# Small TensorE products as two 64-column halves in a 2-block transformer kernel, and a later start of GpSimd's first weight sums

## The reference, cut to what matters

```python
def layer_norm(x, g, b):
    ...
    y = (xf - mu) * lax.rsqrt(var + LN_EPS) * g + b

# RWKV-7 in chunks of 128 tokens, per head (8 heads of 64): with L a masked 128x128
# matrix (row t uses tokens s before t, or up to t),
#   Z = L1 @ V (+ state part),  U = X @ Z,  Y = L2 @ U + L3 @ V (+ state part)

mod = jax.nn.silu(c) @ w_ada + b_ada              # shift2 enters the router as a constant
logits = h2 @ w_router                            # = ... + shift2 @ w_router, the same for all tokens
out = rms_norm_2(x, final_norm_g)                 # needs the sum of squares of each token
```

## Time and profile before

| | |
|---|---|
| median of the runs | 2457.34 us |
| the profiled execution | 2456.72 us |
| its span, first to last instruction | 2454.9 us |
| TensorE busy | 2294.8 us, 93% of the span |
| VectorE, ScalarE, GpSimd busy | 28%, 16%, 16% |
| mean granted TensorE clock | 0.988 |

### The profile page before, as it was taken

One profiled execution on the slowest core, in us unless ns is written; L12 is line 12 of the kernel. 1 busy time (PEld: TensorE's weight loads), 2 busy tenths in 40 slices (PEclk: granted clock), 3 DMA queues, 4 the chain that ended last, 5 costly groups with the idle time before them and its releaser, 6 DMA issues.

```text
span 2454.9 us, 28556 instructions
## 1 busy us (share of the span) xinstructions
PE 2294.8 (93%) x12460; PEld 1536.5 (63%) x12460; DVE 675.2 (28%) x1192; ACT 401.5 (16%) x780; POOL 389.3 (16%) x347
## 2 busy tenths in 40 slices
PE   9999999999999999999888888899999998888878
PEld 8766676676667888987333333378889863333324
DVE  4543224433215644212100000034443221000001
ACT  3310112521014321111100000033112020000001
POOL 2377631258742000000000000000000000000000
PEclk9999999999999999999999999999999999999999
DMA  7377732358742332238999999953333599999997
GB/s 269 115 288 288 305 128 86 110 214 343 298 165 75 108 138 87 104 137 353 412 429 427 428 427 428 415 183 113 113 104 103 201 394 429 427 428 427 428 426 315
DMA packets 136504, 654.61 MB, mean 267 GB/s; under 512 B 9784, under 2 KB 14776, under 8 KB 107832
## 3 DMA queue, kind: packets, MB, share of 16 engines
q1 hardware_dynamic: 136376, 652.71, 66.8%
HBM read 651.64 MB, written 1.05 MB: 266 GB/s over the span
## 4 chain that ended last, share of the span: by engine, by line
PE 72%; DMA 22%; DVE 3%; ACT 1%; issue 1%; SPq 0%; POOL 0%; DVEq 0%; ACTq 0%
PE bank L719 71%; DMA PRGT<-in_w_exp_up 9%; DMA ring<-in_w_exp_up 6%; DMA PRGT<-in_w_exp_down 4%; DMA ring<-in_w_exp_gate 3%; DVE R L1876 1%; ACT R L3055 1%; SPq L639 0%; DVE stat L1857 0%; PE bank L1277 0%; DMA ring<-in_hy_w_in 0%; DVE sm L2002 0%; POOL PRGT L3153 0%; ACT SQ L3095 0%; PE bank L897 0%
## 5 line engine op out<-in xcount | busy, mean ns | idle before, releaser
L719 PE MATMUL bank<-hT,ring 128*128 128x256 f32 x3392 | 759.2, 382 | 7.7 <-ACT hT L2699 7.7
L719 PEld LDWEIGHTS bank<-hT,ring 128*128 128x128 f32 x3392 | 640.7, 191 | 114.9 <-issue 18.6
L719 PE MATMUL bank<-PRGT,R 128*32 128x512 f32 x1120 | 288.8, 608 | 39.2 <-DMA PRGT<-in_w_exp_up 33.1
L719 PE MATMUL bank<-ring,R 128*32 128x512 f32 (+1 forms) x960 | 263.5, 596 | 32.6 <-DMA ring<-in_w_exp_up 17.8
L3229 POOL TENSOR_TENSOR SQ<-xT 128x512 f32<-128x512 f32 x4 | 4.2, 1041 | 1513.9 <-DVE xT L2672 1513.8
L719 PE MATMUL bank<-PRGT,SQ 128*32 128x512 f32 (+2 forms) x896 | 192.0, 533 | 16.1 <-ACT SQ L3095 12.2
L719 PEld LDWEIGHTS bank<-PRGT,R 128*32 128x32 f32 x1120 | 77.6, 112 | 183.1 <-issue 182.6
L719 PEld LDWEIGHTS bank<-ring,R 128*32 128x32 f32 (+1 forms) x960 | 73.2, 114 | 179.6 <-issue 179.3
L719 PE MATMUL bank<-PRGT,ring 128*128 128x256 f32 (+4 forms) x1040 | 175.9, 372 | 0.0
L719 PE MATMUL bank<-ring,SQ 128*32 128x512 f32 (+2 forms) x552 | 161.9, 556 | 8.3 <-ACT SQ L3095 8.3
L719 PEld LDWEIGHTS bank<-PRGT,ring 128*128 128x128 f32 (+3 forms) x1040 | 145.1, 170 | 28.0 <-issue 2.2
(11 more groups left out here) (387 smaller groups left out, 2158.4 us busy)
## 6 DMA issues: line engine op xcount, KB each, us to landing
PRGT<-in_w_exp_gate SPq DMA_DIRECT2D x36, 2048.0 KB, 31.9
PRGT<-in_w_exp_up SPq DMA_DIRECT2D x34, 2048.0 KB, 31.8
ring<-in_mlp_w SPq DMA_DIRECT2D x32, 2048.0 KB, 9.2
PRGT<-in_w_exp_down SPq DMA_DIRECT2D x32, 2048.0 KB, 32.1
ring<-in_w_exp_up SPq DMA_DIRECT2D x30, 2048.0 KB, 31.9
ring<-in_w_exp_gate SPq DMA_DIRECT2D x28, 2048.0 KB, 32.6
PRGT<-in_w_ada SPq DMA_DIRECT2D x32, 1536.0 KB, 11.3
ring<-in_w_exp_down SPq DMA_DIRECT2D x22, 2048.0 KB, 31.9
```

The lines of the kernel that those rows point to most:

```text
L719: return mm(o, lhsT=lhsT, rhs=rhs, start=first, stop=last, **kw)
```

## The change

Four things are done. (1) Each product of the recurrence with a triangular matrix becomes two, by `causal`: the first takes source rows 0 to 63 and writes output rows 0 to 63 (64x64 weights), the second takes all 128 source rows and writes output rows 64 to 127 (weights of 128 rows and 64 columns). The corner of `XT` is then never read, and its memset goes. (2) The 8 products of `rconst` become 16, with 64 weight columns each, to the lower and the upper half. (3) So do the 12 of `sums_by_token`. (4) GpSimd's `weight_sums(l, 0)` waits until VectorE has scaled the eighth tile of the layer norm.

```diff
+                def causal(o, h, lhs, rhs, start, stop, **more):
+
+                    for half in range(2):
+                        src, dst = slice(0, 64 + 64 * half), slice(64 * half, 64 * half + 64)
+                        ins = mul(o[dst, h * 64:h * 64 + 64], lhs[src, place(h) * P + 64 * half:place(h) * P + 64 * half + 64],
+                                  rhs[src, :], start, stop, **more)
+                    return ins
...
                     for h in range(RW_H):
-                        ins = mul(o[:, h * 64:h * 64 + 64], NT[c][:, place(h) * P:(place(h) + 1) * P],
-                                  VT2[:, c * 512 + h * 64:c * 512 + h * 64 + 64], h == 0, False, skip_group_check=True)
+                        ins = causal(o, h, NT[c], VT2[:, c * 512 + h * 64:c * 512 + h * 64 + 64], h == 0, False, skip_group_check=True)
...
                     for h in range(RW_H):
-                        ins = mul(o[:, h * 64:h * 64 + 64], XT[c][:, place(h) * P:(place(h) + 1) * P], Zm[:, h * 64:h * 64 + 64])
+                        ins = causal(o, h, XT[c], Zm[:, h * 64:h * 64 + 64], True, True)
...
-                        hs, hp = slice(h * 64, h * 64 + 64), slice(place(h) * P, (place(h) + 1) * P)
-                        mul(o[:, hs], RB[c][:, hp], Um[:, hs], h == 0, False, skip_group_check=True)
-                        ins = mul(o[:, hs], RK[c][:, hp], VT2[:, c * 512 + h * 64:c * 512 + h * 64 + 64], False, False,
-                                  skip_group_check=True)
+                        causal(o, h, RB[c], Um[:, h * 64:h * 64 + 64], h == 0, False, skip_group_check=True)
+                        ins = causal(o, h, RK[c], VT2[:, c * 512 + h * 64:c * 512 + h * 64 + 64], False, False, skip_group_check=True)
...
                 for k in range(KT):
-                    mul(o[:, 0:36], mod[:, 48 * l + 24 + k:48 * l + 25 + k].to_broadcast([P, P]), wr[:, k, :], k == 0, False)
+                    for half in (slice(0, 64), slice(64, 128)):
+                        mul(o[half, 0:36], mod[:, 48 * l + 24 + k:48 * l + 25 + k].to_broadcast([P, 64]), wr[:, k, :], k == 0, False)
...
                     for tt in range(TT):
-                        ins = mul(acc[3][:, tt:tt + 1], SQ[:, k, tt * P:(tt + 1) * P], C("ones")[:, 0:1],
-                                  first and k == 2 * t and tt == 0, last and k == 2 * t + 1, skip_group_check=True)
+                        for half in (0, 64):
+                            ins = mul(acc[3][half:half + 64, tt:tt + 1], SQ[:, k, tt * P + half:tt * P + half + 64], C("ones")[:, 0:1],
+                                      first and k == 2 * t and tt == 0, last and k == 2 * t + 1, skip_group_check=True)
...
-                for c in range(TT):
-                    v.memset(h8(XT[c])[64:128, :, 0:64], 0.0)
...
                 s, u = SLOT_AT[f"mlp{l}"][2 * (q % 4 // 2) + 1]
                 pool.wait_ge(slot_full[s], loaded(u, q // 4))
+                if q == 0:
+                    pool.wait_ge(sems["norm_scaled"], (8, 30)[l])
```

## The result

The changed kernel takes 2508.77 us (median of 4 runs, 2508.01 to 2508.93), the kernel before 2457.89 beside it (4 runs, 2455.5 to 2461.85). The ratio is 1.021, with a 95% interval of 1.0197 to 1.0222: 2.1% or 51 us slower. The forecast was 2490, with a range up to 2502. The direction was right, and so was the mechanism of the products and of the norms. The loss by TensorE's clock was taken far too small; the forecast was off by 19 us in all, and the time lies 7 us outside the range.

What follows compares the result with a forecast made beforehand. TensorE was taken to bound the kernel, with 72% of the span. 2456.7 + 41.1 (products) + 3 (clock) - 9.7 (norms) - 1.3 (`rconst`) - 0.5 (token sums) = 2489.3, plus 0.6 for the median: 2490 us, range 2437 to 2502.

Steps and rivals of the forecast that it cites:

- What bounds it: Whole span: 72% TensorE, 22% DMA; a later recurrence moves the experts' stage as a whole and hides nothing.
- The products, +41.1: Recurrence: 256 records become 256 halves at 0.26 us, +38.9, plus entries and exits; ends +35.9 and +61.5 us.
- The edges (entry and exit): Between 12 stretches of recurrence products and the big projections: 0.2 us each, less what chunk 0 pays, +2.2 us.
- rival (A): Recurrence: halves of different height run side by side on separate columns, 0.031 us per record; kernel 2436 us; chance 0.18.
- (B): Recurrence: a shape change costs something between, near 0.145 us per half, paid for by the norms; about 2457 us; chance 0.04.
- The clock, +3 with bounds 0 and +10: Recurrence's four 16-product stretches, 8.3 us each: two falls to half clock, each costing up to 1.7 us.
- if the clock falls in all four long stretches: Recurrence's 16-product stretches: named as the next way to fail, after the price of a shape change.
- The layer norms, -9.7: First norm of each layer: scalings without GpSimd beside them gain 3.65 us in the first layer, 6.04 in the second.
- rival (C): Layer norms: products as forecast, but the norms don't speed up; 2500 us; chance 0.04.
- GpSimd's sums had slack: First layer norm: GpSimd's delayed weight sums cost nothing, ending 1.4 us before its row sums could start.
- The small ones: `rconst` in halves -1.3 us over both layers, token sums -0.5 us, removed memsets worth nothing.
- The sum: Whole kernel: profiled 2456.7 us plus all terms gives 2489.3; median of runs 0.6 higher, 2490 us, 1.3% slower.

Runs made afterwards that it cites:

- the wait alone: Only GpSimd's wait for the layer norm's last scaled tile added to the kernel before; 2447.77 us, ratio 0.9965.
- the last version: The changed kernel, but both halves of each triangular product take all 128 source rows and the memsets stay; 2433.61 us, ratio 0.9907 against the kernel before.
- by turns: Only the recurrence's products in alternating halves of 64 and 128 source rows, memsets gone, against the kernel before; 2517.26 us, ratio 1.024.
- half as many changes of shape: Only the recurrence's products in 64- and 128-source-row halves, their order reversed in every second head, against the kernel before; 2499.07 us, ratio 1.0168.
- sorted: Only the recurrence's products halved, all 64-row halves of a stretch before all 128-row ones, against the kernel before; 2463.71 us, ratio 1.0022.

## Why the prediction was right, and where it was wrong

**What bounds it.** Right. The recurrence is one piece of TensorE, and what it lost moved all behind it; the experts' stage kept its length within 1.4 us (449.5 and 450.9 us from norm to norm in layer 1; 451.2 and 449.9 in layer 2, of which the last token sums are 0.7).

**The products, +41.1.** Right. At full clock a half costs 0.257 us (0.514 a product), forecast at 0.26; 128 products 65.8 us for 27.7. The edges (entry and exit) are 0.14 in 12 stretches, 1.7, where I had 2.2. Together +39.8. It was read from two places where shapes change after every pair of records, and it carries over to tiles on disjoint columns: rival (A), the only way to the faster side, is excluded, and (B) too, since it needed 0.145 for a half. The Trainium skill's page "TensorEngine Tiling (Array Packing)", section Key Properties, says that a change of tiling mode drains TensorE while tiles of one mode run independently. The runs agree with both halves of that: 4.11 us with 15 changes and 1.08 with none and neighbours on different columns.

**The clock, +3 with bounds 0 and +10.** This is the step that failed. The two recurrences grew by 31.45 + 31.49 = 62.9 us; less the 39.8 for products and edges, **the clock took 23.1**. I wrote that of the four long stretches two would see a fall of 3.41 us, each costing at most 1.7. All four had one, of 10.2, 10.2, 10.2 and 6.8 us. It began in the stretch and lasted into the big projections behind it. Four more falls, of 3.4 to 6.8 us, came at or behind short stretches, which I had given none. And inside the half-clock time the drained products cost as well, 0.80 against 0.51 each, while I had priced only dense work. I had the shortest falls of the trace as the size of all, though in those places TensorE went back to dense work after a moment, while here the drained stretches of 4 to 10 us come again after 4 to 9 us of dense work. I named the case ("if the clock falls in all four long stretches") as a way to fail, but the upper end of the range, 2502, left only 8 us for it. With 23 in place of 3 the same sum gives 2510. The 23.1 is what the recurrences grew by, less products and edges; some 55 us at half clock stand behind it.

**The layer norms, -9.7.** The mechanism is right: -3.66 and -6.06 between the reciprocals, and -9.6 in a run of its own (interval -12 to -5). So rival (C) is out. That the size agrees to 0.1 us is luck in part. Eight of the kernels, the one before among them, have these norms unchanged, and yet they take 253.4 to 255.7 us in layer 1 and 254.3 to 255.9 in layer 2, by how long the clock was at 0.50 in them: 0, 3.4 or 6.8 us in layer 1, 3.4 or 6.8 in layer 2. The trace that I read had the shortest in the one and the longest in the other. With the wait (the changed kernel, the wait alone and the last version) all six norms take 249.7, with no fall. So the gain is 8 to 11 us, and in the second layer a part of it is the clock that no longer falls. The Trainium skill's "GPSIMD Engine Reference", section Specifications, states that GpSimd shares its SBUF interfaces with VectorE, with contention for VectorE instructions that have two SBUF inputs. The trace agrees: the scaling is such an instruction, and it took 1.02 us beside GpSimd (8.13 / 8) and 0.48 without (3.84 / 8). That GpSimd's sums had slack was right too: 1.4 us worked out, 1.77 of waiting left in the trace.

**The small ones.** `rconst` -1.5 (two times 1.80 to 1.06; forecast -1.3). The token sums gave -0.9, forecast -0.5: from the start of the last ones to VectorE's last reciprocal it is 1.51 us instead of 2.24, and from the start of the first ones, which I had counted at nothing, to that of the last 1.65 instead of 1.79. The memsets were worth nothing, as forecast: from the reciprocal of the second norm to the start of the recurrence it is 213.37 us before and 213.33 after. Another 1.7 came from the clock behind the first `rconst`, which is no effect of the edit.

**The sum** on the profiled spans: +39.8 + 23.1 - 9.7 - 1.5 - 0.9 = +50.8. With the luck behind `rconst`, -1.7, the start, +1.6, and small differences elsewhere it stands against +52.2.

## What to carry to other kernels

Here splitting a product to skip a zero block lost in every order that was tried: 2.4% by turns, 1.7% with half as many changes of shape, 0.2% sorted. The version that computes the zeros (two equal halves on different columns) is 75 us faster than the changed kernel, which skips them. Before an order of tiles is chosen, count the changes of shape, 0.14 us each in this kernel, and see whether neighbours write different columns. Where changes of shape make TensorE wait for itself for microseconds within dense work, price the clock over the whole region and not by the shortest fall in the old trace: at half clock the dense work behind the stretch pays as well, and here the clock was more than a third of what the recurrence lost.

## What the runs showed of the hardware

- The cost of a change between 64-row and 128-row tiles is a constant here, 0.14 us at full clock, although the tiles share no column: 2.15, 3.12 and 4.11 us for 32 records with 1, 8 and 15 changes.
- The same 32 records, all of one shape and on the two column halves by turns, take 1.08 us; on one column half after the other, with one change, 2.15. Two tiles side by side are worth nearly a factor of 2, and a change of shape loses that as well.
- The granted clock fell to 0.5 while the profile showed TensorE busy without a gap; some 27 us in each recurrence, in places for 10 us. The loss by the long and the short stretches together (23.1 us) is more than the sum of the two apart (17.9). What decides exactly when it falls was not isolated.
- A fall of the clock worth 1.7 us behind `rconst` was there in some kernels and not in others that had the same instructions at that place. So it was near the start (nine of eleven kernels) and in the layer norms. One trace against another can be some 2 us off in each of these places.
